# The last attention head's small products between eighths of the head loop's first trip, with no meeting point before it

## What is computed

```python
def memory_cross_attention(q_raw, mem_n, w_kv):
    k, v = jnp.split(mem_n @ w_kv, 2, axis=-1)          # 256 x 1024 each
    ...
    scores = jnp.einsum('bshd,bmhd->bhsm', q, k).astype(jnp.float32) * (XA_HEAD_DIM ** -0.5)
    p = jax.nn.softmax(scores, axis=-1).astype(v.dtype)
    o = jnp.einsum('bhsm,bmhd->bshd', p, v)

o_c = memory_cross_attention(q_c, rmsnorm(mem, mem_norm_g[l]), w_kv_mem[l])
p_c = (o_c * jax.nn.silu(z_c)) @ w_br_c[l]
```

## Time and profile before

| | |
|---|---|
| median of 3 runs | 2278.49 us |
| lowest and highest run | 2278.01, 2280.3 us |
| the profiled execution, its own time | 2280.22 us |
| span of its trace | 2278.5 us |
| mean granted TensorE clock | 0.991 |
| TensorE matmuls busy | 2201.8 us, 97% of the span |
| VectorE, ScalarE, POOL busy | 1235.0, 802.2, 721.9 us |
| DMA | 249.76 MB, mean 110 GB/s |

### The profile page before, as it was taken

One profiled execution on the slowest core, in us unless ns is written; L12 is line 12 of the kernel. 1 busy time (PEld: TensorE's weight loads), 2 busy tenths in 40 slices (PEclk: granted clock), 3 DMA queues, 4 the chain that ended last, 5 costly groups with the idle time before them and its releaser, 6 DMA issues.

```text
span 2278.5 us, 29625 instructions
## 1 busy us (share of the span) xinstructions
PE 2201.8 (97%) x10616; PEld 1782.0 (78%) x10616; DVE 1235.0 (54%) x1543; ACT 802.2 (35%) x1035; POOL 721.9 (32%) x550
## 2 busy tenths in 40 slices
PE   5999998999999999999999999999999999999998
PEld 4888886888778778787787787777877888888887
DVE  5533232247776676666766777667533343555333
ACT  5533231343343343333434334325334222222223
POOL 0000000037375374673744746636420100010000
PEclk9999998999999999999999999999999999999999
DMA  6344342333323323232332232333344656463334
GB/s 217 83 126 125 102 119 66 106 104 84 90 75 84 86 83 90 75 86 81 87 83 81 83 90 78 83 81 102 93 115 146 197 171 186 145 185 120 116 116 148
DMA packets 374921, 249.76 MB, mean 110 GB/s; under 512 B 21369, under 2 KB 349250, under 8 KB 373826
## 3 DMA queue, kind: packets, MB, share of 16 engines
q1 hardware_dynamic: 357106, 197.40, 31.4%
q0 software_dynamic: 10832, 38.80, 5.1%
q10 hardware_dynamic: 6912, 12.59, 1.5%
HBM read 221.50 MB, written 27.26 MB: 109 GB/s over the span
## 4 chain that ended last, share of the span: by engine, by line
PE 88%; DVE 6%; DMA 2%; issue 2%; ACT 1%; SPq 0%; DVEq 0%; POOLq 0%; ACTq 0%
PE bank L426 25%; PE bank L428 25%; PE bank L427 24%; PE bank L902 2%; PE bank L915 2%; PE bank L985 1%; DVE wl L420 1%; PE bank L986 1%; DVE kc L1745 1%; DMA raw<-in_w_in_dram 1%; PE bank L994 1%; DVE vc L1745 1%; PE bank L924 1%; PE bank L794 1%; PE bank L779 1%
## 5 line engine op out<-in xcount | busy, mean ns | idle before, releaser
L426 PE MATMUL bank<-uh,wh 128*128 128x512 f32 x2048 | 834.5, 407 | 30.0 <-DVE wl L420 25.1
L428 PE MATMUL bank<-uh,wl 128*128 128x512 f32 x2048 | 804.2, 393 | 0.0
L427 PE MATMUL bank<-ul,wh 128*128 128x512 f32 x2048 | 800.0, 391 | 0.0
L420 DVE TENSOR_TENSOR wl<-raw,wh 128x1024 fp32r<-128x1024 f32 x352 | 465.9, 1328 | 535.4 <-ACT wh L412 534.6
L412 ACT ACTIVATE wh<-raw 128x1024 fp32r<-128x1024 f32 x352 | 370.3, 1057 | 617.1 <-DMA raw<-in_w_in_dram 223.7
L426 PEld LDWEIGHTS bank<-uh,wh 128*128 128x128 f32 x2048 | 386.3, 189 | 140.3 <-issue 45.4
L428 PEld LDWEIGHTS bank<-uh,wl 128*128 128x128 f32 x2048 | 385.7, 188 | 85.4
L427 PEld LDWEIGHTS bank<-ul,wh 128*128 128x128 f32 x2048 | 386.9, 189 | 77.0 <-issue 4.5
L599 POOL TENSOR_TENSOR hr<-tcos,gr 128x512 f32<-128x512 f32 x32 | 49.5, 1546 | 313.1 <-DVE gi L1867 312.9
L555 POOL DMA_DIRECT2D gated_c<-ox x8 | 4.5, 564 | 363.0 <-DVE ox L1608 362.5
L1314 ACT ACTIVATE gk<-bank 128x512 f32<-128x512 f32 x48 | 28.7, 598 | 208.6 <-PE bank L428 208.5
(11 more groups left out here) (313 smaller groups left out, 3015.6 us busy)
## 6 DMA issues: line engine op xcount, KB each, us to landing
raw<-in_w_in_dram SPq DMA_DIRECT2D x224, 512.0 KB, 3.8
raw<-in_w_kv_mem_dram SPq DMA_DIRECT2D x32, 512.0 KB, 3.8
raw<-in_w_out_dram SPq DMA_DIRECT2D x32, 512.0 KB, 3.8
gates<-gk ACTq DMA_DIRECT2D x48, 256.0 KB, 4.4
gates<-gates POOLq DMA_DIRECT2D x24, 512.0 KB, 4.7
raw<-in_s_w_glu_dram SPq DMA_DIRECT2D x16, 512.0 KB, 3.9
raw<-in_w_br_c_dram SPq DMA_DIRECT2D x16, 512.0 KB, 3.8
raw<-in_w_br_a_dram SPq DMA_DIRECT2D x16, 512.0 KB, 3.8
```

The lines of the kernel that those rows point to most:

```text
L420: dve.tensor_tensor(k.wl[slot][:, c], k.raw[slot][:, c], k.wh[slot][:, c].bitcast(F32), ALU.subtract).then_inc(k.w_lo, 1)
L426: pe.matmul(o, ah, bh, start=start, stop=False)
L427: pe.matmul(o, ah, bl, start=False, stop=False)
L428: return pe.matmul(o, al, bh, start=False, stop=stop)
```

## The change

TensorE's attention trips now issue three eighths of block b, then `at_small(j, b)`, then the other five (before: the products first, then the whole block). The products of the last head get the same place in the first six blocks of the head loop's first trip. The first meeting point and the separate tail are gone from all engines. What it guarded is done by counts: `w_used` at M_FREE, which is the end of the last trip's memory blocks, for POOL's fills and SyncE's S5 loads; `xa_st0`, `xa_st1` (the stores of ox have landed) before the second loop trip on ScalarE and VectorE and before POOL's first `mixer`; `xa_og` on TensorE. The tiles that the first loop trip and the S5 loads write move to the front of the area, where mh and ml lie; zk and rq, which it does not write, come behind. On ScalarE and VectorE the last head's exps and small work move behind the splits of the loop's first blocks.

```diff
             k.vc = sb(area, "vc", [S])
-            k.rq = sb(area, "rq", [S])
             k.rk = sb(area, "rk", [S])
             k.zs = sb(area, "zs", [S])
+            k.zbs = sb(area, "zbs", [S])
+            k.cwh = sb(area, "cwh", [CONV, 3])
+            k.braw = sb(area, "braw", [2, 4, GS])
+            k.craw = sb(area, "craw", [2, NS])
+            k.bpad = sb(area, "bpad", [2, 4, 2, GS])
+            k.rq = sb(area, "rq", [S])
...
+M_FREE = 2 * (B_MIX - 4)
...
     mixer_loads((0, 0))
-    sp.wait_ge(k.phase_end, 4)
+    sp.wait_ge(k.w_used, M_FREE)
     s5_loads((0, 0))
...
-    with pool.Fori(0, XH) as i:
+    with pool.Fori(0, XH - 1) as i:
         attention_store((i, 0))
-    pool.wait_ge(k.xa_st0, 16 * XH)
-    pool.wait_ge(k.xa_st1, 16 * XH)
-    end_phase(k, pool, 1)
-
+    pool.wait_ge(k.w_used, M_FREE)
     for t in (k.qraw, k.kraw, k.vraw):
...
+    attention_store((XH, -1))
     gate_store((0, 0))
+    pool.wait_ge(k.xa_st0, 16 * XH)
+    pool.wait_ge(k.xa_st1, 16 * XH)
     mixer((0, 0), None)
...
-    for b in range(8):
-        at_small((0, 0), b)
-        at_big((1, 0), b)
+    def attention(a, j):
+        for b in range(8):
+            at_big(a, b, range(3))
+            at_small(j, b)
+            at_big(a, b, range(3, 8))
+
+    attention((1, 0), (0, 0))
     with pe.Fori(2, XH) as i:
-        for b in range(8):
-            at_small((i, -1), b)
-            at_big((i, 0), b)
-    for n in range(6):
-        at_small((XH, -1), n)
-    end_phase(k, pe, 1)
+        attention((i, 0), (i, -1))
...
-    mixer((0, 0), None, None)
+    pe.wait_ge(k.xa_out, 8 * XH - 1)
+    for b in range(PER):
+        if b == 1:
+            pe.wait_ge(k.xa_out, 8 * XH)
+        big((0, 0), b, *range(3))
+        at_small((XH, -1), b)
+        big((0, 0), b, *range(3, 8))
+    pe.wait_ge(k.xa_og, 2 * XH)
     mixer((1, 0), (0, 0), None)
...
-    attention(None, (XH, -1))
-    end_phase(k, act, 1)
...
-    def mixer(a, j, l, gate=None, blocks=PER):
+    def mixer(a, j, l, gate=None, blocks=PER, x=None):
 
         def end_of(b):
+            if x and b < 2: at_exp(x, 2 * b); at_exp(x, 2 * b + 1)
...
-    mixer((0, 0), None, None)
+    mixer((0, 0), None, None, x=(XH, -1))
+    act.wait_ge(k.xa_st0, 16 * XH)
+    act.wait_ge(k.xa_st1, 16 * XH)
...
-    attention(None, (XH, -1))
-    end_phase(k, dve, 1)
...
                 split_lo(k, dve, B_MIX + b + 1, PER, a, [half])
+            if x and half: at_small(x, b)
```

More of the change, by code:

```diff
@@ L211, in build @@
             k.st = sb(area, "st", [P])
-            k.cwh = sb(area, "cwh", [CONV, 3])
             k.hph = sb(area, "hph", [4, NT])
@@ L217, in build @@
             k.xb = sb(area, "xb", [S])
-            k.braw = sb(area, "braw", [2, 4, GS])
-            k.craw = sb(area, "craw", [2, NS])
             k.bt = sb(area, "bt", [6, 4, GS])
-            k.bpad = sb(area, "bpad", [2, 4, 2, GS])
             k.cpad = sb(area, "cpad", [2, 2, NS])
@@ L236, in build @@
             k.pt = sb(area, "pt", [S])
-            k.zbs = sb(area, "zbs", [S])
         with ExitStack() as area:
@@ L653, in pool_program @@
     pool.wait_ge(k.g_st, 16 * HEADS)
-    end_phase(k, pool, 2)
+    end_phase(k, pool, 1)
     pool.dma_start(k.yst[:, :, :], k.y_d.rearrange("(t p) s -> p t s", p=P)).then_inc(k.y_in, 16)
@@ L1083, in tensor_program @@
         big((HEADS + 1, 0), 2 + b, *range(8))
-    pe.wait_ge(k.phase_end, 8)
+    pe.wait_ge(k.phase_end, 4)
     def glu(j):
@@ L1443, in scalar_program @@
     mixer((HEADS + 1, 0), None, (HEADS, -1), gate=PER, blocks=2)
-    end_phase(k, act, 2)
+    end_phase(k, act, 1)
     split_hi(k, act, B_GT + 13)
@@ L1872, in s5_sum, with mixer @@
         stt(k.ma[:, :], k.xb[:, :], k.dh[:, 0:1], ps[5][:, :], ALU.mult, ALU.add).then_inc(k.ysum, 1)
-    def mixer(a, j, l, blocks=PER, heads=True):
+    def mixer(a, j, l, blocks=PER, heads=True, x=None):
         def split(b, half):
@@ L1925, in vector_program @@
     dve.wait_ge(k.pad_zero, 4)
-    mixer((0, 0), None, None)
+    mixer((0, 0), None, None, x=(XH, -1))
+    dve.wait_ge(k.xa_st0, 16 * XH)
+    dve.wait_ge(k.xa_st1, 16 * XH)
     mixer((1, 0), (0, 0), None)
@@ L1931, in vector_program @@
     mixer((HEADS + 1, 0), None, (HEADS, -1), 2, False)
-    end_phase(k, dve, 2)
+    end_phase(k, dve, 1)
     split_lo(k, dve, B_GT + 13)
```

## The result

| | before | changed |
|---|---|---|
| median of the runs, us | 2279.08 (4 runs, 2278.01 to 2280.3) | 2256.31 (4 runs, 2255.06 to 2256.63) |
| ratio, 95% interval | | 0.9899 [0.9882, 0.9916] |
| profiled execution, us (its span) | 2280.22 (2278.5) | 2256.02 (2254.3) |

The change makes the kernel 22.8 us faster; by the interval of the ratio the gain lies between 19 and 27 us. The forecast was 24.5 us, 2254.0.

The account below looks back on a forecast made before the run. TensorE was taken as the bound, with 88% of the chain. Seam 15.5 us (21.6 + 2.15 - 8.2) plus trips 9.0 made 24.5 us, giving 2254.0 us after adjusting to the median; range 2251 to 2261.5.

Parts of the forecast that it names:

- Seam removed: Between last attention block and head loop: 21.6 us up to the first matmul go, plus 2.15 us of low clock.
- Seam added: The last head's small products between eighths of the loop's first six blocks cost 8.2 us, ends 7.4 and 10.6.
- Seam moved: The tail's work, 4.2 us on ScalarE and 7.6 on VectorE, is hidden in the loop's first trip.
- Rival B: Part of the seam's stall returns in the loop's first trip, two split waits of 5.0 us: 2264 us; chance 0.04.
- Trips: In the three attention trips TensorE's eight waits for zx, exp and ptx close: 9.0 us, ends 0 and 9.0.
- C: Attention trips, blocks 2 to 4: waiting products delay buffer release, load and split, feeding itself; 20.5 us slower, 2299; chance 0.03.
- D: Loop's first trip: bank changes and short products between eighths lower the clock; slower, 2316 us; chance 0.02.
- E: Some engine still meets the others, so the change doesn't do what it says: 2278.5 us; chance 0.01.

Follow-up runs that it names:

- the run of the trips alone: Kernel before with only TensorE's new order inside the attention trips, tail and meeting point kept: 2272.16 us, ratio 0.9966, 8.1 us faster.
- behind six eighths: Changed kernel with the attention trips' small products behind each block's sixth eighth instead of the third: 2260.32 us, ratio 0.9906.
- the seam without trips: Changed kernel with the attention trips back in their old order on TensorE, run twice: 2268.6 us (ratio 0.9947) and 2265.93 us (0.9935).

## Why the prediction was right

**Seam removed.** Forecast 21.6 and 2.15 us; the loop's first matmul moved from 21.81 behind the last attention block to 0.23, and no stretch around it has a lower clock. As forecast.

**Seam added.** Forecast 8.2 us, with ends 7.4 and 10.6. By starts: 1.98 for transposes and first scores, 1.55 for the other scores, 0.36 and 0.35 for the two turns, 3.04 for the output, together 7.28. Behind them the first big matmul has 0.42, 0.41, 0.31, 0.31 and 0.63 us to the next start, which is 0.93 over plain spacings of 0.23. That makes 8.2 us. The upper end with the slow output group did not come. The Trainium skill's rule ("TensorE: Matmul & The Clock Gate", section "Part 4: PE-mode transpose"), by which transposes don't count for the full clock, would have shown as a lower clock; in the loop's first trip it is 1.00 throughout, with transposes in three of its blocks (L774 at 345.47, L787 at 382.11 and 393.49). Each of these groups takes 0.35 to 0.44 us among dense matmuls, so the trip says nothing on transposes that stand alone.

**Seam moved.** ScalarE and VectorE took the last head's work into the loop's first trip, and TensorE waits for nothing in it: the 70 us of slack held. Rival B is refuted.

**Trips.** Forecast 9.0 us, measured 8.2 by the trace and 8.1 by the run of the trips alone. All eight waits are closed, the narrow ones too: the exp whose cover was put at 0.2 us and the split at 0.7. The term was 0.8 too large: the 9.0 is the sum of the gaps and takes for granted that the blocks between them keep their length, and some did not. The 96 matmuls of 256 columns between the last scores and the first turn, before, in trips 2 and 3:

```profile
206.43:217.50 11.07, 11.07 (x98) 11.04 (x97) 5.64 (x11) 4.85 (x9) 0.00 (x0) 1.00 0.52 144
283.41:294.91 11.50, 11.50 (x98) 11.47 (x97) 6.06 (x12) 6.02 (x10) 0.00 (x0) 1.00 0.51 147
```

and in the second trip of the changed kernel:

```profile
203.94:215.44 11.50, 11.50 (x98) 11.47 (x97) 6.68 (x12) 6.42 (x12) 0.00 (x0) 1.00 0.54 152
```

The spacing is 0.120 in place of 0.115 us, with no idle time recorded in either. The forecast read its 0.12 in the third trip, where these blocks had it already; in the first two they had 0.115. Those two trips lose 0.4 us each. Why the spacing differs was not tried.

**C and D.** C, the wait that feeds itself, is refuted twice: it does not arise here, and behind six eighths it arises and stays single. D, the clock, is refuted by the 1.00 of the loop's first trip; changes of bank between eighths cost 0.08 to 0.40 us of handover each and no clock. The Trainium skill's rule for D ("TensorE: Matmul & The Clock Gate", section "A second HAM failure mode: psum-queue depth-cycling") tells of short idle times between the groups of matmuls; in this trip TensorE has none, and the clock of 1.00 does not bear the rule out here. E is refuted by the timeline.

**The sum.** Between the two profiled executions lie 24.2 us, against 24.5 forecast: 15.3 and 8.2 by the steps above, and 0.7 more behind the seam, which the forecast had not counted. So it is in part luck that the sum is only 0.3 off. The 0.7 has two parts. The loop's seven steps from one L849 to the next are 0.25 us shorter each, 1.7 together, with five clock falls in either profile: of the last six, those with a fall take 149.9 to 150.0 us before and in the run of the trips alone, and 149.6 to 149.8 in every kernel with the seam's edit and the split where it was. That gain comes with the seam's edit; which part of it makes it (the places of the tiles, the counts, the code) was not tried. Behind the loop 1.0 us is lost, mostly in TensorE's one long wait for wl, 5.9 us instead of 5.0. The median came out 2.3 us above the forecast all the same: 1.7 of it was taken off because the profiled execution of before lay that far above its median, and the changed kernel's lies 0.3 below its own. Of two profiles that agree with the sum, one being high is no reason for the other to be.

## What to carry to other kernels

- Where one engine's queue is in order and the bound, put a product that depends on other engines a few eighths into the next block: far enough behind its input, and far enough ahead of what is released after it. Both distances could be read here from the trace before the edit (0.2 and 0.7 us of cover), and the place that is right is where neither wait appears.
- A meeting point costs more than the wait that it shows. Its parts here were the wait for POOL and its stores (5.1 us), the low clock, which cost some 1.1 us more in the tail and 1.7 behind it, and the small products that had nothing big queued between them (7.3).
- Look at a bound engine's short waits by the clock that follows them, too. Seven waits of 2.9 us, for a split that stood behind work nobody waited for, cost 30 us and not 20, and one line moved took them away.

## What the runs showed of the hardware

The granted clock fell in most cases, not in all, behind a short standstill of TensorE among dense matmuls. Behind the seven waits of 2.89 to 3.02 us in the changed kernel's profile it was 0.57 to 0.66 over the next 4 us in five cases and 1.00 in two; in the nine profiles that have such waits (2.83 to 3.03 us) it fell behind 47 of 63. Behind the waits of 2.71 and 2.24 us in the first attention trip (the seam without trips, two runs) it was 0.59 and 0.57; behind the wait of 2.0 us at the same place in the kernel before it stayed 1.00, and so it did behind 1.27 and 1.42 us with the products behind six eighths. Only in the tail, where short products and gaps had followed each other for some 8 us, did it fall behind a wait of 1.89. At the trips' starts a fall costs 1.6 us beyond the wait. What decides between the cases of equal length stays open. It may be why trips, and so runs, of one kernel differ by 1 to 2 us; that was not tried by itself.
